# Four weight sums per pair of a three-stage FFN, made by VectorE between its low parts instead of by accumulating DMAs

## The chip, the cores and the metric

The kernel runs on one core of one Trainium2 chip. The metric is the device time of one execution in microseconds (us), the median of several runs. Beside it stands one profiled execution of the same kernel, from which all rows come. A core has TensorE (matmuls, in PSUM), VectorE and ScalarE (element by element), GpSimd (POOL) and SyncE (SP), each with an instruction list of its own that it works off in order; semaphores are the only order between the lists. Transfers are done by 16 DMA engines.

## The reference

Two transformer-like blocks on 512 tokens of width 2048, in FP32. The first is a mixer of pooling and a state space model, the second an attention block with a gated FFN. The change lies in that FFN alone:

```python
D_MODEL, SEQ = 2048, 512
D_FF = -(-8 * D_MODEL // (3 * 256)) * 256          # 5632

h = rmsnorm_2(x, g_pre_ffn[l]) * (1.0 + sc_f) + sh_f
f = (jax.nn.silu(h @ w_gate[l]) * (h @ w_up[l])) @ w_down[l]
x = x + gt_f * rmsnorm_2(f, g_post_ffn[l])
```

## The kernel before

**Tiling.** `D_FF` is 44 tiles of 128 hidden channels. For each tile the kernel needs 128 columns of `w_gate` (g) and of `w_up` (u), each as a RAW tile of 128 x 2048 (16 blocks of 128 input channels). The first two tiles (`PLAIN`) are computed directly. The other 42 (`FAST`) take g and u as the two columns of a 2 x 2 block matrix (input channels in two halves of 1024, tokens in two halves of 256) and use the seven-product scheme of fast matrix multiplication: 7 products of 128 x 1024 weights instead of 8. One such tile is called a pair here, since it has a gate and an up part.

**Seven weights of a pair.** `weight(s2, j)` gives them. With g1, g2, u1, u2 for the halves of g and u they are: 0: g1; 1: sum 3 = g1 + u1; 2: sum 1 = u1 + u2 (made in place of u1); 3: g2; 4: sum 2 = sum 3 + u2; 5: u2; 6: sum 4 = g2 + sum 2 (made in place of g2). The sums' numbers are those of the names `sum_1` to `sum_4` in the code. Two RAW buffers alternate between even and odd pairs.

**High and low parts.** TensorE multiplies at reduced precision (`fp32r`), so each weight is split. ScalarE makes the high part (`hi_part`, line 1177, into `QH`), VectorE the low part (`lo_part`, line 2618, weight minus high part, into `QL`). There are four slots. The high part of weight j + 3 may start when product j - 1 is done (`q_done`), since it takes that product's slot; it also waits for its sum. The low part waits for the high part (`q_hi`), and TensorE's product waits for the low part (`q_lo`).

**Products.** On TensorE (`fast_pair`, lines 1749 and 1751) each product is 8 times a matmul of 512 columns with the high part and one of 256 columns with the low part. Banks of PSUM are shared by products: product 3 goes into the bank of product 0 after ScalarE copied that (`p1_copied`, line 1181), product 5 into that of product 1, and product 6 into that of product 2, after VectorE's subtraction `r` (line 2639) has read it (`taken`).

**VectorE's list for a pair s**, in its order: low part of weight 5; low part of 6; `r` (2639); low part of weight 0 of pair s + 1; low part of 1; line 2642, a drain, line 2644; low part of 2; line 2647; low part of 3; line 2651, a drain, line 2654 (the sum of the gate part, which ScalarE's silu waits for), line 2655 (the sum of the up part); low part of weight 4 of pair s + 1; a drain; line 2661, the multiply into `FO`. ScalarE's list after the high part of weight 3: silu (`gated`, line 1190), the copy of product 0 of the next pair, the high part of weight 4, then of 5, a copy of product 1.

**Sums before.** GpSimd issues them as accumulating DMAs: a DMA with `accum_op=ALU.add` adds its source onto its destination in SBUF. `sum_3` adds u1 onto a `SUMS` tile into which SP had loaded g1 a second time from HBM (0.5 MB); `sum_1` adds u2 onto u1; `sum_2` waits until the low part of weight 1 is made, and `sum_4` until that of weight 3 is. ScalarE's high parts 1, 2, 4 and 6 wait for `first_sums` and `later_sums`.

**Before and after the pairs.** At the start, VectorE also makes the low parts of the combined tokens (`TA`, `TB`, `TC`) and the `FO` multiply of the second plain tile (`plain_hidden(1)`, line 2613), on whose `out_read` TensorE's first product waits. After the pairs comes the multiplication with `w_down` (lines 1779 to 1781).

Of the kernel before, what the change touches and what calls it, by code (L numbers as in the profile page):

```python
# [24 lines left out]
P = 128  # L25
# [125 lines left out]
def build(nc, w_units, w_ada, c_row, x_t, p_t, vec_d, con_d, mask_d, ssm_par, ssm_bc, w_pool_d,  # L151
# [117 lines left out]
    QL = at("QL", 32 * K, [P, 4, FULL_K * P], FP32R)  # L269
    SUMS = [at("SUM0", T0 + 9696, [P, FULL_K * P]), at("SUM1", T0 + 3040, [P, FULL_K * P])]  # L270

# [20 lines left out]
    def weight(s2, j):  # L292

        g, u, h = RAWS[s2][:, 0, :], RAWS[s2][:, 1, :], FULL_K * P
        return [g[:, 0:h], SUMS[s2][:, :], u[:, 0:h], g[:, h:2 * h], SUMS[s2][:, :], u[:, h:2 * h], g[:, h:2 * h]][j]

# [6 lines left out]
    with ExitStack() as ctx:  # L303
        PS = ctx.enter_context(nc.psum_tensor("PS", [P, 8, S], FP32))

        def sem(name):
# [46 lines left out]
        pair_loaded = [sem("pair_loaded0"), sem("pair_loaded1")]  # L353
        first_sums, later_sums, q_hi, q_lo, q_done, copied, taken = (
            sem(n) for n in ("first_sums", "later_sums", "q_hi", "q_lo", "q_done", "copied", "taken"))
        t_sum, t_hi, t_lo, gate_summed, up_summed, silu_done, f_made = (
# [10 lines left out]
        def _(sp):  # L367
# [80 lines left out]
            for k in (1, 0):  # L448
                sp.dma_start(RAWS[1][:, k, :], w_units[U_FFN + 2 * PLAIN + 2 + k]).then_inc(pair_loaded[1], 16)
            sp.dma_start(SUMS[0][:, :], w_units[U_FFN + 2 * PLAIN, :, 0:FULL_K * P]).then_inc(pair_loaded[0], 16)  # L450
            for k in range(2):
# [3 lines left out]
            hidden_saved(0, f_d[0], 0)  # L455
            sp.wait_ge(f_made, PLAIN)
            sp.dma_start(SUMS[1][:, :], w_units[U_FFN + 2 * PLAIN + 2, :, 0:FULL_K * P]).then_inc(pair_loaded[1], 16)
            with sp.Fori(0, LOOPED // 4) as i:
                for e in range(4):
                    for k in (1, 0):  # L460

                        sp.wait_ge(q_lo, 28 * i + (Q0 + PRODUCTS * e + 7 - k))
                        sp.dma_start(RAWS[e % 2][:, k, :], w_units[bass.ds(8 * i + (U_FFN + 2 * PLAIN + 2 * e + 4 + k), 1)]
                                     .rearrange("a p n -> p (a n)")).then_inc(pair_loaded[e % 2], 16)
                    sp.dma_start(SUMS[e % 2][:, :], w_units[bass.ds(8 * i + (U_FFN + 2 * PLAIN + 2 * e + 4), 1), :, 0:FULL_K * P]
                                 .rearrange("a p n -> p (a n)")).then_inc(pair_loaded[e % 2], 16)
                    hidden_saved(4 * i + (e + 1), f_d[bass.ds(4 * i + (e + 1), 1)].rearrange("a p n -> p (a n)"),
                                 (e + 1) % 2)
# [43 lines left out]
        def _(gp):  # L512
# [76 lines left out]
            def sum_1(s, r):

                u = RAWS[r][:, 1, :]
                gp.wait_ge(first_sums, 32 * s + 16)
                gp.dma_start(u[:, 0:h], u[:, h:2 * h], accum_op=ALU.add).then_inc(first_sums, 16)

            def sum_2(s, r):

                gp.wait_ge(q_lo, PRODUCTS * s + (Q0 + 2))
                gp.dma_start(SUMS[r][:, :], RAWS[r][:, 1, h:2 * h], accum_op=ALU.add).then_inc(later_sums, 16)

            def sum_4(s, r):  # L600

                gp.wait_ge(q_lo, PRODUCTS * s + (Q0 + 4))
                gp.wait_ge(later_sums, 32 * s + 16)
                gp.dma_start(RAWS[r][:, 0, h:2 * h], SUMS[r][:, :], accum_op=ALU.add).then_inc(later_sums, 16)

            def weight_sums(s, e, loaded):

                r, n = e % 2, (e + 1) % 2
                sum_2(s, r)
                gp.wait_ge(first_sums, 32 * s + 32)  # L610
                sum_3(n, loaded)
                sum_4(s, r)
                sum_1(s + 1, n)

            sum_3(0, 48)
            sum_1(0, 0)
            for s in range(FAST - 1):
                weight_sums(s, s % 2, 48 * ((s + 1) // 2 + 1))
            sum_2(LOOPED + 1, 1)
            sum_4(LOOPED + 1, 1)  # L620

# [213 lines left out]
        def _(act):  # L835
# [334 lines left out]
            def hi_part(s, s2, j, slot, done):  # L1170

                act.wait_ge(q_done, done)
                if j in (1, 2):
                    act.wait_ge(first_sums, 32 * s + 16 * j)
                if j in (4, 6):
                    act.wait_ge(later_sums, 32 * s + 16 * (j // 2 - 1))
                act.activation(QH[:, slot, :], weight(s2, j), ACT.Copy).then_inc(q_hi, 1)  # L1177
# [55 lines left out]
            plain_silu(1)  # L1233
            act.wait_ge(pair_loaded[0], 48)
            for j in range(2):
# [12 lines left out]
            with act.Fori(0, LOOPED // 4) as i:  # L1248
                for e in range(4):
                    fast_pair(4 * i + e, e, 96 * i + 48 * ((e + 1) // 2 + 1))  # L1250
            fast_pair(LOOPED, 0, 48 * (LOOPED // 2 + 1))
            fast_pair(LOOPED + 1, 1, 0, False)
# [534 lines left out]
        def _(v):  # L1787
# [834 lines left out]

            def fast_pair(s, e, saved, more=True):
                s2, n2, b0 = e % 2, (e + 1) % 2, 4 - 4 * (e % 2)
# [65 lines left out]
            for t in range(FULL_K):  # L2690
                m = 3 * DT + FULL_K + t
                ins = v.scalar_tensor_tensor(out=TC[:, t, hi], in0=RES[:, FULL_K + t, hi], scalar=MOD[:, m:m + 1],
                                             in1=f32(TC[:, t, lo]), op0=ALU.add, op1=ALU.subtract)
            ins.then_inc(t_lo, 1)
            lo_part(0, 0, 3, 3)
            lo_part(0, 0, 4, 0)
            with v.Fori(0, LOOPED // 4) as i:
                for e in range(4):
                    fast_pair(4 * i + e, e, 32 * i + 16 * (e // 2 + 1))
            fast_pair(LOOPED, 0, 8 * LOOPED + 16)  # L2700
            fast_pair(LOOPED + 1, 1, 8 * LOOPED + 16, False)

# [193 lines left out]
```

## Time and profile before

| | us |
|---|---|
| median of 3 runs | 3140.84 |
| lowest and highest | 3133.31, 3145.36 |
| profiled execution | 3136.03 |
| its span in the trace | 3134.3 |
| TensorE busy | 3078.4 |
| VectorE busy | 2070.9 |
| ScalarE busy | 1157.4 |
| mean granted clock of TensorE | 0.992 |

The profile gives each engine's busy time, the instructions in order of time with their start, duration and the idle time ahead of them, and for each idle time what ended it. "PE" is TensorE, "DVE" VectorE, "ACT" ScalarE, "POOL" GpSimd. A duration runs from start to the last write; the next instruction of the same engine can start a little before it ends, so that the step from start to start is what counts in a full list. The granted clock is the share of 2.4 GHz that TensorE gets; 0.5 is 1.2 GHz.

### The profile page before, as it was taken

The page shows a single profiled execution, that of the slowest core. Times are in us where ns is not written, and L with a number is a line of the kernel's source. Part 1 is how long each engine was busy: PE and PEld are TensorE (multiplying, and loading weights), DVE is VectorE, ACT ScalarE, POOL GpSimd, SP SyncE. Part 2 cuts the span into 40 slices and gives each one's busy share as a digit, 9 for nine tenths or more (in the row PEclk, how much of TensorE's full clock was granted, in tenths as well). Part 3 has the DMA queues.
Part 4 walks back from the last instruction along what each step waited for, and adds up shares of the span by engine and source line. Part 5 has one row for each costly group of instructions (what it writes and reads, how often), then busy time and mean ns, then how long its engine had stood idle before and what let it go on. Part 6 is the DMA issues. An engine that isn't in the chain of part 4 may idle for free.

```text
span 3134.3 us, 41612 instructions
## 1 busy us (share of the span) xinstructions
PE 3078.4 (98%) x15416; PEld 2569.8 (82%) x15416; DVE 2070.9 (66%) x2743; ACT 1157.4 (37%) x1522; POOL 417.0 (13%) x589
## 2 busy tenths in 40 slices
PE   8999999999999999999999899999999998999998
PEld 7888877888878888888787688888888887888887
DVE  6666556868885444555788866666666666666665
ACT  5323343213233333444623444444444443222223
POOL 0111100111100000000011311111111111122113
PEclk9999999999999999999999899999999999999999
DMA  4444454875752222222386499999999997455544
GB/s 187 145 136 122 127 194 178 297 270 211 272 226 92 82 81 75 75 80 80 121 304 232 158 238 251 265 252 251 251 250 250 252 254 212 173 187 187 188 166 170
DMA packets 136410, 591.07 MB, mean 189 GB/s; under 512 B 24096, under 2 KB 24368, under 8 KB 99056
## 3 DMA queue, kind: packets, MB, share of 16 engines
q1 hardware_dynamic: 69968, 343.18, 30.7%
q0 software_dynamic: 62448, 218.45, 26.5%
q10 hardware_dynamic: 3888, 28.03, 2.3%
q8 instruction: 67, 1.10, 0.1%
q14 instruction: 39, 0.32, 0.0%
HBM read 457.19 MB, written 37.76 MB: 158 GB/s over the span
## 4 chain that ended last, share of the span: by engine, by line
PE 95%; DVE 3%; DVEq 0%; DMA 0%; ACT 0%; issue 0%; SPq 0%; ACTq 0%
PE PS L1749 18%; PE PS L1329 15%; PE PS L1331 15%; PE PS L1330 15%; PE PS L1751 9%; PE PS L1779 5%; PE PS L1781 5%; PE PS L1780 5%; PE PS L1598 1%; PE PS L1625 1%; PE PS L1382 1%; PE PS L1383 1%; PE PS L1384 1%; PE PS L1613 1%; PE PS L1495 0%; PE PS L1454 0%
## 5 line engine op out<-in xcount | busy, mean ns | idle before, releaser
L1329 PE MATMUL PS<-XHL,WH 128*128 128x512 f32 x1968 | 775.2, 394 | 5.6 <-DVE WL L1791 2.6
L1331 PE MATMUL PS<-XHL,WL 128*128 128x512 f32 x1968 | 766.2, 389 | 0.0
L1330 PE MATMUL PS<-XHL,WH 128*128 128x512 f32 x1968 | 766.0, 389 | 0.0
L839 ACT ACTIVATE WH<-RAW 128x2048 fp32r<-128x2048 f32 x138 | 263.9, 1912 | 522.0 <-PE PS L1331 513.7
L1329 PEld LDWEIGHTS PS<-XHL,WH 128*128 128x128 f32 x1968 | 369.4, 188 | 94.1 <-issue 13.7
L1331 PEld LDWEIGHTS PS<-XHL,WL 128*128 128x128 f32 x1968 | 369.4, 188 | 77.4
L1330 PEld LDWEIGHTS PS<-XHL,WH 128*128 128x128 f32 x1968 | 369.5, 188 | 77.0 <-issue 2.2
L1791 DVE TENSOR_TENSOR WL<-RAW,WH 128x2048 fp32r<-128x2048 f32 x138 | 316.5, 2294 | 79.8 <-ACT WH L839 79.7
L1749 PE MATMUL PS<-XHL,QH 128*128 128x512 f32 x1008 | 361.6, 400 | 2.7 <-DVE FO L2613 2.7
L2618 DVE TENSOR_TENSOR QL<-RAW,QH 128x1024 fp32r<-128x1024 f32 x210 | 257.0, 1224 | 110.4 <-ACT QH L1177 110.4
L1177 ACT ACTIVATE QH<-RAW 128x1024 fp32r<-128x1024 f32 x210 | 221.3, 1058 | 259.7 <-PE PS L1751 231.2
L1751 PE MATMUL PS<-XHL,QL 128*128 128x256 f32 x1008 | 283.8, 282 | 0.0
L1779 PE MATMUL PS<-WH,FH 128*128 128x512 f32 x704 | 274.9, 391 | 8.6 <-issue 8.6
L1780 PE MATMUL PS<-WL,FH 128*128 128x512 f32 x704 | 274.8, 390 | 0.0
L1781 PE MATMUL PS<-WH,FL 128*128 128x512 f32 x704 | 274.8, 390 | 0.0
L1749 PE MATMUL PS<-TA,QH 128*128 128x512 f32 x672 | 239.3, 399 | 0.0
L1749 PEld LDWEIGHTS PS<-XHL,QH 128*128 128x128 f32 x1008 | 190.1, 189 | 50.6 <-issue 3.1
L1826 DVE CUSTOM_DVE_ANT_0 ADA<-ADA,CB 128x1024 f32<-128x1024 f32 x192 | 226.1, 1221 | 5.8 <-DMA ADA<-w_ada_dram 5.8
L1262 ACT ACTIVATE WH<-RAW 128x2048 fp32r<-128x2048 f32 x44 | 84.2, 1915 | 336.5 <-PE PS L1781 336.5
L1751 PEld LDWEIGHTS PS<-XHL,QL 128*128 128x128 f32 x1008 | 191.2, 190 | 0.0
L2618 DVE TENSOR_TENSOR QL<-SUM,QH 128x1024 fp32r<-128x1024 f32 x84 | 102.9, 1225 | 132.3 <-ACT QH L1177 132.3
L1751 PE MATMUL PS<-TA,QL 128*128 128x256 f32 x672 | 188.7, 281 | 0.0
(369 smaller groups left out, 4603.4 us busy)
## 6 DMA issues: line engine op xcount, KB each, us to landing
RAW<-w_units_dram SPq DMA_DIRECT2D x268, 1024.0 KB, 4.9
ADA<-w_ada_dram POOLq DMA_DIRECT2D x192, 512.0 KB, 5.5
SUM<-RAW POOLq DMA_DIRECT2D x84, 512.0 KB, 5.1
SUM<-w_units_dram SPq DMA_DIRECT2D x42, 512.0 KB, 7.4
RAW<-RAW POOLq DMA_DIRECT2D x42, 512.0 KB, 5.3
RAW<-SUM POOLq DMA_DIRECT2D x42, 512.0 KB, 4.6
FR<-f_dram SPq DMA_DIRECT2D x11, 1024.0 KB, 5.5
spill_dram<-SIG POOLq DMA_DIRECT2D x24, 256.0 KB, 2.3
```

Source lines behind the costliest of these rows:

```text
L839: act.activation(WH[:, slot, :], RAW[:, slot, :], ACT.Copy).then_inc(hi_ready, 1)
L1329: pe.matmul(PS[:, bank, :], wh, rh[:, x, :], start=k == 0, stop=False)
L1330: pe.matmul(PS[:, bank, :], wh, rl[:, x, :], start=False, stop=False)
L1331: ins = pe.matmul(PS[:, bank, :], wl, rh[:, x, :], start=False, stop=k == n - 1)
L1749: pe.matmul(in_halves(PS[:, bank, :]), wh, x, start=k == 0 and j not in (3, 5, 6), stop=False, skip_group_check=True)
L1751: ins = pe.matmul(PS[:, bank, 0:HALF_S], wl, x[:, 0, :], start=False, stop=k == FULL_K - 1, skip_group_check=True)
L1779: pe.matmul(PS[:, 4 + n % 4, :], fh, wh, start=k == 0, stop=False, skip_group_check=True)
L1780: pe.matmul(PS[:, 4 + n % 4, :], fh, wl, start=False, stop=False, skip_group_check=True)
L1781: ins = pe.matmul(PS[:, 4 + n % 4, :], fl, wh, start=False, stop=k == FF_CHUNK - 1, skip_group_check=True)
L1791: v.tensor_tensor(WL[:, slot, :], RAW[:, slot, :], f32(WH[:, slot, :]), ALU.subtract)\
L1826: v.tensor_tensor_reduce(ADA[slot][:, :], ADA[slot][:, :], CB[:, :], 1.0, 0.0, ALU.mult, ALU.add, (MODH if half else MOD)[:, t:t + 1]).the ...
L2618: v.tensor_tensor(QL[:, slot, :], weight(s2, j), f32(QH[:, slot, :]), ALU.subtract).then_inc(q_lo, 1)
```

## The change

The accumulating DMAs on GpSimd and the second load of g1 on SP are gone. VectorE makes the four sums as `tensor_tensor` adds of 128 x 1024: `sum_4` behind the low part of weight 5, `sum_3` of the next pair behind that of 6, `sum_1` behind the next pair's 0, `sum_2` behind the next pair's 2. Both sum tiles are now shared by all pairs: `SUM3` holds g1 + u1, and `SUM2`, which was summed in place, is a tile of its own. One semaphore `sum_ready` takes the place of two. In pair 0, `sum_3` and `sum_1` stand ahead of the low parts 0 and 1, and `sum_2` behind the token parts `TC`. The loads' count per buffer falls from 48 to 32.

```diff
+NEED_SUM = {1: 1, 2: 2, 4: 3, 6: 4}
-    SUMS = [at("SUM0", T0 + 9696, [P, FULL_K * P]), at("SUM1", T0 + 3040, [P, FULL_K * P])]
+    SUM3 = at("SUM3", T0 + 9696, [P, FULL_K * P])
+    SUM2 = at("SUM2", T0 + 3040, [P, FULL_K * P])
...
-                    sp.dma_start(SUMS[e % 2][:, :], w_units[bass.ds(8 * i + (U_FFN + 2 * PLAIN + 2 * e + 4), 1), :, 0:FULL_K * P]
-                                 .rearrange("a p n -> p (a n)")).then_inc(pair_loaded[e % 2], 16)
...
-            def sum_3(r, loaded):
-
-                g, u = RAWS[r][:, 0, :], RAWS[r][:, 1, :]
-                gp.wait_ge(pair_loaded[r], loaded)
-                gp.dma_start(SUMS[r][:, :], u[:, 0:h], accum_op=ALU.add).then_inc(first_sums, 16)
...
-            for s in range(FAST - 1):
-                weight_sums(s, s % 2, 48 * ((s + 1) // 2 + 1))
...
             def hi_part(s, s2, j, slot, done):
 
                 act.wait_ge(q_done, done)
-                if j in (1, 2):
-                    act.wait_ge(first_sums, 32 * s + 16 * j)
-                if j in (4, 6):
-                    act.wait_ge(later_sums, 32 * s + 16 * (j // 2 - 1))
+                if j in NEED_SUM:
+                    act.wait_ge(sum_ready, 4 * s + NEED_SUM[j])
...
+            def sum_3(r, loaded):
+                v.wait_ge(pair_loaded[r], loaded)
+                v.tensor_tensor(SUM3[:, :], RAWS[r][:, 0, 0:FULL_K * P], RAWS[r][:, 1, 0:FULL_K * P], ALU.add)\
+                 .then_inc(sum_ready, 1)
+
+            def sum_1(r):
+                u, h = RAWS[r][:, 1, :], FULL_K * P
+                v.tensor_tensor(u[:, 0:h], u[:, 0:h], u[:, h:2 * h], ALU.add).then_inc(sum_ready, 1)
+
+            def sum_2(r):
+                v.tensor_tensor(SUM2[:, :], SUM3[:, :], RAWS[r][:, 1, FULL_K * P:], ALU.add).then_inc(sum_ready, 1)
+
+            def sum_4(r):
+                a12 = RAWS[r][:, 0, FULL_K * P:]
+                v.tensor_tensor(a12, a12, SUM2[:, :], ALU.add).then_inc(sum_ready, 1)
...
+                    if j == 2:
+                        sum_4(s2)
+                    if j == 3 and more:
+                        sum_3(n2, loaded)
+                    if j == 4 and more:
+                        sum_1(n2)
+                    if j == 6 and more:
+                        sum_2(n2)
...
             v.tensor_tensor(TB[:, :, hi], RES[:, b, lo], f32(TB[:, :, lo]), ALU.subtract).then_inc(t_lo, 1)
+            sum_3(0, 32)
+            sum_1(0)
             for j in range(2):
                 lo_part(0, 0, j, j)
             plain_hidden(1)
...
             ins.then_inc(t_lo, 1)
+            sum_2(0)
             lo_part(0, 0, 3, 3)
```

## Rows read from the trace of the kernel before

**Rows 1.** The page's first part: busy time of each engine.

```profile
PE 3078.4 (98%) x15416; PEld 2569.8 (82%) x15416; DVE 2070.9 (66%) x2743; ACT 1157.4 (37%) x1522; POOL 417.0 (13%) x589
```

**Rows 2.** TensorE's instructions in order of time: start us, us, engine, line, operation.

```profile
1802.46 0.69 PE L1749 MATMUL PS<-XHL,QH 128*128 128x512 f32 x1 [2.70 <-DVE FO L2613]
...
1806.91 0.40 PE L1749 MATMUL PS<-TA,QH 128*128 128x512 f32 x1
...
2202.65 0.40 PE L1749 MATMUL PS<-TA,QH 128*128 128x512 f32 x1
...
2635.01 0.28 PE L1751 MATMUL PS<-XHL,QL 128*128 128x256 f32 x1
```

**Rows 3.** The waits from 1802 to 2640 us, TensorE's (all of them).

```profile
PE PS L1749 <- DVE FO L2613: 2.7, 1, 2.7
```

**Rows 4.** Busy time of each engine in one stretch, with the header.

```profile
core 0: us, PE busy (x) PEld busy (x) DVE busy (x) ACT busy (x) POOL busy (x), PEclk, DMA share, GB/s
1806.80:2634.80 828.00, 828.00 (x4689) 717.96 (x4688) 563.44 (x626) 385.61 (x457) 143.45 (x169) 1.00 0.96 251
```

**Rows 5.** VectorE's instructions in order of time, one pair in mid-stretch.

```profile
2201.11 1.23 DVE L2618 TENSOR_TENSOR QL<-RAW,QH 128x1024 fp32r<-128x1024 f32 x1 [0.93 <-ACT QH L1177]
2202.25 0.68 DVE L2651 TENSOR_TENSOR ST<-PS,ST 128x512 f32<-128x512 f32 x1
2203.11 0.69 DVE L2654 TENSOR_TENSOR ST<-ST 128x512 f32<-128x512 f32 x1 [0.17 <-issue]
...
2205.94 1.23 DVE L2618 TENSOR_TENSOR QL<-SUM,QH 128x1024 fp32r<-128x1024 f32 x1 [1.53 <-ACT QH L1177]
2207.32 0.69 DVE L2661 TENSOR_TENSOR FO<-ST 128x512 f32<-128x512 f32 x1 [0.16 <-issue]
2207.93 1.22 DVE L2618 TENSOR_TENSOR QL<-RAW,QH 128x1024 fp32r<-128x1024 f32 x1
2209.67 1.23 DVE L2618 TENSOR_TENSOR QL<-RAW,QH 128x1024 fp32r<-128x1024 f32 x1 [0.52 <-ACT QH L1177]
2210.82 0.68 DVE L2639 TENSOR_TENSOR ST<-ST,PS 128x512 f32<-128x512 f32 x1
...
2216.47 0.68 DVE L2642 TENSOR_TENSOR ST<-PS,ST 128x512 f32<-128x512 f32 x1
2217.24 0.69 DVE L2644 TENSOR_TENSOR ST<-ST 128x512 f32<-128x512 f32 x1
```

**Rows 6.** ScalarE's instructions in order of time, the same pair.

```profile
2203.83 0.64 ACT L1190 ACTIVATE ST<-ST 128x512 f32<-128x512 f32 x1 [2.75 <-DVE ST L2654]
2204.37 0.58 ACT L1181 ACTIVATE ST<-PS 128x512 f32<-128x512 f32 x1
2204.85 1.05 ACT L1177 ACTIVATE QH<-SUM 128x1024 fp32r<-128x1024 f32 x1
```

**Rows 7.** DMA issues: count, KB each, median us from issue to landing.

```profile
RAW<-w_units_dram SPq DMA_DIRECT2D x268, 1024.0 KB, 4.9
```

**Rows 8.** VectorE's instructions in order of time, ahead of the first product.

```profile
1799.16 1.22 DVE L2618 TENSOR_TENSOR QL<-RAW,QH 128x1024 fp32r<-128x1024 f32 x1
1800.29 1.22 DVE L2618 TENSOR_TENSOR QL<-SUM,QH 128x1024 fp32r<-128x1024 f32 x1
1801.43 0.68 DVE L2613 TENSOR_TENSOR FO<-PS,SIG 128x512 f32<-128x512 f32 x1
```

**Rows 9.** Busy time in three short stretches, columns as in rows 4.

```profile
732.00:736.00 4.00, 4.00 (x18) 3.31 (x19) 4.00 (x5) 2.66 (x2) 0.00 (x0) 1.00 0.01 4
740.00:744.00 4.00, 4.00 (x20) 3.30 (x19) 1.21 (x3) 0.94 (x2) 1.06 (x2) 1.00 0.94 312
1802.00:1806.00 4.00, 3.54 (x11) 3.06 (x12) 2.55 (x6) 2.48 (x4) 0.66 (x1) 0.57 0.63 139
```

**Rows 10.** TensorE's instructions in order of time, behind another stop.

```profile
731.84 0.50 PE L1329 MATMUL PS<-XHL,WH 128*128 128x512 f32 x1 [1.46 <-DVE BB L2266]
```

**Rows 11.** Line 2618, plain weights: shortest/median/longest ns, first and last start.

```profile
L2618 DVE TENSOR_TENSOR QL<-RAW,QH x210: 1216/1225/1228, 1799.2 to 2625.4; 128x1024 fp32r<-128x1024 f32 x105
```

More of the change, by code:

```diff
@@ L294, in weight @@
         g, u, h = RAWS[s2][:, 0, :], RAWS[s2][:, 1, :], FULL_K * P
-        return [g[:, 0:h], SUMS[s2][:, :], u[:, 0:h], g[:, h:2 * h], SUMS[s2][:, :], u[:, h:2 * h], g[:, h:2 * h]][j]
+        return [g[:, 0:h], SUM3[:, :], u[:, 0:h], g[:, h:2 * h], SUM2[:, :], u[:, h:2 * h], g[:, h:2 * h]][j]
     def f32(ap):
@@ L353, in build @@
         pair_loaded = [sem("pair_loaded0"), sem("pair_loaded1")]
-        first_sums, later_sums, q_hi, q_lo, q_done, copied, taken = (
-            sem(n) for n in ("first_sums", "later_sums", "q_hi", "q_lo", "q_done", "copied", "taken"))
+        sum_ready, q_hi, q_lo, q_done, copied, taken = (
+            sem(n) for n in ("sum_ready", "q_hi", "q_lo", "q_done", "copied", "taken"))
         t_sum, t_hi, t_lo, gate_summed, up_summed, silu_done, f_made = (
@@ L449, in _ @@
                 sp.dma_start(RAWS[1][:, k, :], w_units[U_FFN + 2 * PLAIN + 2 + k]).then_inc(pair_loaded[1], 16)
-            sp.dma_start(SUMS[0][:, :], w_units[U_FFN + 2 * PLAIN, :, 0:FULL_K * P]).then_inc(pair_loaded[0], 16)
             for k in range(2):
@@ L455, in _ @@
             hidden_saved(0, f_d[0], 0)
-            sp.wait_ge(f_made, PLAIN)
-            sp.dma_start(SUMS[1][:, :], w_units[U_FFN + 2 * PLAIN + 2, :, 0:FULL_K * P]).then_inc(pair_loaded[1], 16)
             with sp.Fori(0, LOOPED // 4) as i:
@@ L579, in _ @@
                 gp.tensor_tensor(BB[:, t, :], BB[:, t, :], RES[:, t, :], ALU.add).then_inc(x3_ready, 1)
-            h = FULL_K * P
-            def sum_3(r, loaded):
-                g, u = RAWS[r][:, 0, :], RAWS[r][:, 1, :]
-                gp.wait_ge(pair_loaded[r], loaded)
-                gp.dma_start(SUMS[r][:, :], u[:, 0:h], accum_op=ALU.add).then_inc(first_sums, 16)
[L589 to L616, printed above, removed]
-            for s in range(FAST - 1):
-                weight_sums(s, s % 2, 48 * ((s + 1) // 2 + 1))
-            sum_2(LOOPED + 1, 1)
-            sum_4(LOOPED + 1, 1)
             def ada_load(n):
@@ L1233, in _ @@
             plain_silu(1)
-            act.wait_ge(pair_loaded[0], 48)
+            act.wait_ge(pair_loaded[0], 32)
             for j in range(2):
@@ L1249, in _ @@
                 for e in range(4):
-                    fast_pair(4 * i + e, e, 96 * i + 48 * ((e + 1) // 2 + 1))
-            fast_pair(LOOPED, 0, 48 * (LOOPED // 2 + 1))
+                    fast_pair(4 * i + e, e, 64 * i + 32 * ((e + 1) // 2 + 1))
+            fast_pair(LOOPED, 0, 32 * (LOOPED // 2 + 1))
             fast_pair(LOOPED + 1, 1, 0, False)
@@ L2621, in both, with fast_pair @@
                 return (ST[:, a, i:i + 2, HALF_S:S] for a in range(2))
-            def fast_pair(s, e, saved, more=True):
+            def sum_3(r, loaded):
[10 more added lines that the diff above has]
+                v.tensor_tensor(a12, a12, SUM2[:, :], ALU.add).then_inc(sum_ready, 1)
+            def fast_pair(s, e, saved, loaded, more=True):
                 s2, n2, b0 = e % 2, (e + 1) % 2, 4 - 4 * (e % 2)
@@ L2698, in _ @@
                 for e in range(4):
-                    fast_pair(4 * i + e, e, 32 * i + 16 * (e // 2 + 1))
-            fast_pair(LOOPED, 0, 8 * LOOPED + 16)
-            fast_pair(LOOPED + 1, 1, 8 * LOOPED + 16, False)
+                    fast_pair(4 * i + e, e, 32 * i + 16 * (e // 2 + 1), 64 * i + 32 * ((e + 1) // 2 + 1))
+            fast_pair(LOOPED, 0, 8 * LOOPED + 16, 16 * LOOPED + 32)
+            fast_pair(LOOPED + 1, 1, 8 * LOOPED + 16, 0, False)
             def down_lo(n):
```

## The prediction

> **What bounds the kernel now.** I began with the busy shares: TensorE is busy for 98% of the span, VectorE for 66% [rows 1]. So time can go only where TensorE stops, and it can come only where something new stops it. The stretch that the change touches is found next, by the first and the last matmul of the fast pairs: they run from 1802.46 to 2635.01 us, 833 of 3134 us for 42 pairs [rows 2]. The list of waits then says what TensorE waited for there: one entry, 2.7 us before the very first product, for the `FO` multiply of VectorE [rows 3]. In the stretch from 1806.8 to 2634.8 us TensorE is busy for all of the 828 us, at a granted clock of 1.00, while VectorE has work for 563 us of them and the DMA engines for 0.96 of their time [rows 4]. Product 1 of the first pair begins at 1806.91, and the last matmul ends at 2635.29 [rows 2]: 828.38 us for 42 x 7 - 1 = 293 products are 2.827 us each, and 19.79 us for a pair. No accumulating DMA is late for TensorE. Taking these DMAs away can therefore give it nothing, and everything hangs on whether VectorE still keeps up.
>
> **Why the busy share misleads.** VectorE is busy for 563.4 / 828 x 19.79 = 13.5 us of a pair [rows 4]; four adds of 1.22 us would make it 18.4, still below 19.8. But VectorE's list is in order, and at two places it must wait for ScalarE. So I laid one pair out, name by name, as a ring of starts, beginning at the GATE add (line 2654) and ending at that of the next pair. The pair shown starts at 2199.82 (its product 1 at 2202.65 [rows 2], less one product), so GATE, at 2203.11, starts 3.29 us into a pair [rows 5].
>
> **Terms that the trace shows.** From GATE to the `lo` of weight 4: 2203.11 to 2205.94, 2.83 us. Inside lie ScalarE's silu, its copy of product 0 and its `hi` of weight 4, end to end [rows 6], and VectorE idles 1.5 us. This piece can't shrink when VectorE is late, for the silu starts 0.03 us after GATE ends. Then `lo` 4 to `FO` 1.38, `FO` to `lo` 5 0.61. Sum 4.82 us [rows 5].
>
> **Sum of weight 6 (sum_4), the one with a price of its own.** It stands behind `lo` 5 and ahead of `lo` 6, and ScalarE's `hi` 6 waits for it, which `lo` 6 waits for in turn. Before, `hi` 6 had its sum from a DMA and waited only for TensorE. Now: `lo` 5 to sum_4 1.14, sum_4 itself 1.22, hand-over 0.03, `hi` 1.06, hand-over 0.04, in all 3.50 us from `lo` 5 to `lo` 6, against 1.74 before [rows 5, 6]. VectorE idles over 1.1 us of it, with everything behind it queued: sum_3, the subtraction `r` (line 2639), on which product 6 waits, and the next pair's low parts.
>
> **The other three sums.** sum_3, sum_1 and sum_2 have no wait of their own that is late: the RAW tiles of the next pair are asked for after `lo` 5 and `lo` 6 of the pair before, about 20 us ahead of sum_3, and land in 4.9 us [rows 7]. The two loads that remain lose only SUM loads ahead of or behind them on SP's queue, which nobody waits for any more. Each sum costs its pitch. No row shows a plain f32 add of 128x1024, but the low part is the same instruction form at the same size, and three VectorE instructions back to back started 1.13 and 1.14 us apart [rows 8]; I take 1.14. The bounds: 1024 columns cost 1.14 and 512 cost 0.61, so 512 more cost 0.53, and an add without any fixed part 1.06; an add that is in nobody's shadow costs its full duration, 1.225 [rows 11].
>
> The Trainium skill, page "VectorE: DVE Perf Modes", section "The DRAIN you can't avoid", says that the next operation does not start until the pipe is empty. By that each full-width step would cost 1.225 and not 1.14, nine of them 0.77 us more per pair, and the result would be some +74 us; rows 8 show the earlier start, so the sum goes by 1.14.
>
> **The rest of the ring.** Full-width steps behind `lo` 6: `lo` 6, sum_3, `lo` 0, sum_1, `lo` 1, `lo` 2, sum_2, `lo` 3, eight times 1.14 = 9.12 us. Narrow steps: `r` 0.61, line 2642 0.77 (with its drain), line 2644 0.61, line 2647 0.61, line 2651 to GATE 0.86, sum 3.46 us [rows 5]. At each of them I looked at whether ScalarE or TensorE is later than VectorE. `hi` 0 to `hi` 3 need products 3 to 6 done and sum_3 or sum_1; all come over 1 us before VectorE gets there. So the ring is 4.82 + 3.50 + 9.12 + 3.46 = **20.90 us**, against TensorE's 19.79. It isn't covered: 1.11 us per pair too long, and TensorE will run at VectorE's pace.
>
> **When it starts to bite.** TensorE's tightest wait is product 6 on `r`: `r` ends 4.82 + 3.50 + 1.14 + 1.14 + 0.69 = 11.29 after GATE, 14.6 into the pair, and product 6 begins at 16.96. That slack of 2.3 us is used up in two or three pairs. Product 3 waits for the copy of product 0, with 3.3 us of slack, and comes second. In the last pair sum_3 is missing, so `r` is 1.14 earlier and the slack that counts is 3.4. From the GATE of pair 0 to that of pair 40 there are 40 rounds: 40 x 1.11 = 44.4, less 3.4 = **+41.0 us**.
>
> **The start.** sum_3 and sum_1 of pair 0 stand ahead of `lo` 0, `lo` 1 and the `FO` multiply, without an idle place between them, and this `FO` is what TensorE's first product waited for [rows 3, 8]. So TensorE starts 2 x 1.14 = **2.3 us** later. sum_2 of pair 0 lies beside product 1. TensorE had stood 2.7 us, the next 4 us had a mean clock of 0.57, most of it at 1.2 GHz [rows 9], and product 0 took 4.45 instead of 2.83 us [rows 2]. A stop of 5 us may lengthen that by up to another 1.3 us. I take nothing for it and keep it for the range.
>
> **The end.** After the last product the chain (line 2651, GATE, silu, `FO`, `FH`, `FL`) is as before; the loads for the next stage are asked for earlier against TensorE's end than is needed. Nothing.
>
> **POOL and DMA.** 168 accumulating DMAs, 0.5 MB each, and 42 SUM loads go. Does anything run faster for it? `lo` took 1216 to 1228 ns with DMA at 0.96 [rows 4, 11], so VectorE isn't slowed by it; and TensorE issued 18 matmuls in 4 us with DMA at 0.01 and 20 with 0.94 [rows 9]. Nothing, with a bound of 0.01 us per full-width step.
>
> **Sum.** +41.0 + 2.3 = +43.3 us. The profiled execution took 3136.0 us (span 3134.3), which is 4.8 below the median of the runs, 3140.8. So it gives 3179.3 from the profile, 3184 from the median; I say **3181 us**.
>
> **Rivals.**
> (a) *The adds are hidden* (the other side, not slower). Place: the two idle stretches of VectorE, 1.5 and 1.1 us. Price: only the start, +2.3 us, 3138 to 3143. It decides at a ring of 19.79 us, so 1.11 us would have to be missing: four adds of 0.86 instead of 1.14 each, or a `hi` 6 that overlapped sum_4. For it stands that VectorE has 265 us without work in 828 [rows 4]; against it that the wait list gives the order, and that no instruction of this kind and width is under 1.2 us [rows 11]. 7%.
> (b) *The clock falls.* The ring makes TensorE stand about 1.1 us per pair, split between product 6 and product 3. If each stop brought as much of the low clock as the start had, a pair would lose the 1.6 us that product 0 lost, and TensorE would need 21.4 us for it, 0.5 more than the ring: up to 42 x 0.5 = 21 us more, 3185 to 3205. Against it: a stop of 1.46 us at 731.84 was followed by a clock of 1.00; for it: after 2.7 us it fell [rows 9, 10]. 6%.
> (c) *Less DMA makes TensorE or its feeders quicker*, with the ring short enough to let it through: 3115 to 3125. TensorE never waits for DMA, so only its pace could gain, and rows 9 show none. 2%.
> (d) *A longer ring*: an unseen wait of 0.1 to 0.3 us per pair (semaphore hand-over for the new waits in ScalarE, loop branch in VectorE, which today hides in the idle places), 4 to 12 us more: 3185 to 3196. 20%. The change not doing what it says is part of this: if sum_3 did wait for its load on VectorE, all behind it would wait as well; 20 us against 4.9 speaks against it.
>
> **Chances.** The forecast with its own range of 3172 to 3190: 65%; (d) 20%; (a) 7%; (b) 6%; (c) 2%. A tenth of a us in the ring is 4 us in the result, and the runs of before lie 12 us apart. The range of 8 in 10 takes in the forecast and most of (d): 3165 to 3196. A measurement of this kernel can tell about 0.5%, 15.7 us, from no change. Slower by more: the forecast, (d) and (b), 91%; same: (a), 7%; faster: 2%.
>
> **What would show it.** TensorE's wait list gets a new entry, line 1749 for `ST` of line 2639, about 40 times 0.8 to 1.1 us, perhaps a smaller one for ScalarE's copy (line 1181); TensorE's busy time stays, its share falls to about 97%. VectorE's list shows about 1.1 us of idle before `lo` 6 and 1.5 us before `lo` 4, none elsewhere, and GATE adds 20.9 us apart. The first product starts near 1804.8 us. If the GATE adds stay 19.8 us apart, the ring is wrong and (a) holds; if TensorE's clock in the stretch is under 0.98, (b) does.

## The result, and the profile after

The changed kernel takes 3177.54 us (median, 3177.13 to 3178.21), beside 3138.16 for the kernel before in the same job: +39.4 us by the medians (1.3%). The ratio estimated from all the executions is 1.0112, with an interval of 1.0092 to 1.0132; every ratio below is meant in this way, against the kernel before in the same job. The forecast was 3181 us, from +43.3. The profiled execution after took 3177.13 us with a span of 3175.4, 41.1 more than before.

The page's first line, of after, answers to [rows 1]: TensorE's busy time is 10 us up and its share down by a point, VectorE gains 178 us, POOL loses 143.

```profile
PE 3088.3 (97%) x15416; PEld 2566.6 (81%) x15416; DVE 2248.4 (71%) x2911; ACT 1149.1 (36%) x1522; POOL 273.8 (9%) x421
```

TensorE's waits (engine and line, whom for: us in total, times, longest), of after; `L1703` is the product's matmul (1749 before), `L2617` the subtraction `r` (2639), `L2567` the `FO` multiply (2613). Against [rows 3] the first entry is new, and the last has grown from 2.7 to 5.0. The middle one stands behind the pairs, where the multiplication with `w_down` begins; the kernel before has it too, with the same 8.6 us.

```profile
PE PS L1703 <- DVE ST L2617: 29.2, 37, 1.0
...
PE PS L1733 <- issue: 8.6, 1, 8.6
...
PE PS L1703 <- DVE FO L2567: 5.0, 1, 5.0
```

The busy time of the engines over the pairs, of after, columns as in rows 4. VectorE works 733 of 863 us (before 563 of 828), the DMA share is 0.33 instead of 0.96, and the clock is still 1.00.

```profile
1812.00:2675.00 863.00, 833.07 (x4659) 710.53 (x4658) 732.91 (x785) 374.72 (x455) 1.36 (x3) 1.00 0.33 114
```

VectorE's instructions in order of time, of after, one round of the ring; it answers to [rows 5]. `L2572` is a low part, `L2632` GATE, `L2639` `FO`, `L2591` sum_4, `L2579` sum_3, `L2617` `r`.

```profile
2204.63 0.69 DVE L2632 TENSOR_TENSOR ST<-ST 128x512 f32<-128x512 f32 x1 [0.16 <-issue]
...
2207.46 1.23 DVE L2572 TENSOR_TENSOR QL<-SUM,QH 128x1024 fp32r<-128x1024 f32 x1 [1.53 <-ACT QH L1131]
2208.98 0.69 DVE L2639 TENSOR_TENSOR TMP<-ST 128x512 f32<-128x512 f32 x1 [0.30 <-issue]
2209.59 1.22 DVE L2572 TENSOR_TENSOR QL<-RAW,QH 128x1024 fp32r<-128x1024 f32 x1
2210.73 1.22 DVE L2591 TENSOR_TENSOR RAW<-RAW,SUM 128x1024 f32<-128x1024 f32 x1
2213.08 1.23 DVE L2572 TENSOR_TENSOR QL<-RAW,QH 128x1024 fp32r<-128x1024 f32 x1 [1.13 <-ACT QH L1131]
2214.22 1.22 DVE L2579 TENSOR_TENSOR SUM<-RAW 128x1024 f32<-128x1024 f32 x1
2215.36 0.68 DVE L2617 TENSOR_TENSOR ST<-ST,PS 128x512 f32<-128x512 f32 x1
...
2225.60 0.69 DVE L2632 TENSOR_TENSOR ST<-ST 128x512 f32<-128x512 f32 x1 [0.16 <-issue]
```

Read it so: from the low part at 2209.59 to the one at 2213.08 it is 3.49 us, with sum_4 between and then 1.13 us of idle time in which ScalarE makes the high part 6. The other place without work is the 1.53 us ahead of 2207.46. There is no third of more than 0.3 us. GATE to GATE is 20.97 us here, 20.82 for the pair before, and 834.9 / 40 = 20.87 on average, from 1828.83 (pair 0) to 2663.75 (pair 40). ScalarE's own row shows who it waited for, and TensorE's row the stop that this makes at product 6:

```profile
2211.98 2.01 ACT L1131 ACTIVATE QH<-RAW 128x1024 fp32r<-128x1024 f32 x2 [3.12 <-DVE RAW L2591]
```

```profile
2216.09 0.50 PE L1703 MATMUL PS<-XHL,QH 128*128 128x512 f32 x1 [0.82 <-DVE ST L2617]
```

**Where the 41.1 us of the two traces are.** From the first matmul of the pairs to the end of the last: before 2635.29 - 1802.46 = 832.8, after 2677.14 - 1803.00 = 874.1, +41.3 us. The stop ahead of them: 2.70 to 4.97, +2.3. What lies ahead of that stop was 1.7 us shorter in this execution and what lies behind the pairs 0.7 shorter. I put both down to scatter: in before_again_1 below, a second trace of the unchanged kernel, the first matmul of the pairs comes at 1804.44 and not at 1802.46. Sum 41.2, for the 41.1 of the spans.

### The profile page after: what moved, and what is told of

Its sections match the earlier page's. It is cut to its first block, busy times and chain, and to the rows that moved or that the text cites. A ratio compares the mean times of both kernels' runs of the same rounds, so it can differ in the third digit from the quotient of the medians.

```text
span 3175.4 us, 41477 instructions
## 1 busy us (share of the span) xinstructions
PE 3088.3 (97%) x15416; PEld 2566.6 (81%) x15416; DVE 2248.4 (71%) x2911; ACT 1149.1 (36%) x1522; POOL 273.8 (9%) x421
## 4 chain that ended last, share of the span: by engine, by line
PE 69%; DVE 19%; DVEq 5%; issue 4%; ACT 3%; DMA 0%; ACTq 0%
PE PS L1283 15%; PE PS L1285 14%; PE PS L1284 14%; DVE QL L2572 7%; PE PS L1733 5%; PE PS L1735 5%; PE PS L1734 5%; ACT QH L1131 3%; DVEq L2621 2%; DVEq L2630 2%; DVE SUM L2579 2%; DVE RAW L2591 1%; DVE SUM L2587 1%; PE PS L1552 1%; PE PS L1579 1%
## 5 line engine op out<-in xcount | busy, mean ns | idle before, releaser
L1703 PE MATMUL PS<-XHL,QH 128*128 128x512 f32 x1008 | 367.4, 406 | 34.9 <-DVE ST L2617 29.2
L2572 DVE TENSOR_TENSOR QL<-RAW,QH 128x1024 fp32r<-128x1024 f32 x210 | 256.1, 1220 | 49.6 <-ACT QH L1131 49.5
L1131 ACT ACTIVATE QH<-RAW 128x1024 fp32r<-128x1024 f32 x210 | 213.7, 1053 | 206.5 <-DVE RAW L2591 126.3
L1703 PEld LDWEIGHTS PS<-XHL,QH 128*128 128x128 f32 x1008 | 190.2, 189 | 98.6 <-DVE ST L2617 40.3
L1703 PE MATMUL PS<-TA,QH 128*128 128x512 f32 x672 | 237.7, 397 | 0.0
L2701 DVE TENSOR_TENSOR RES<-RES,PS 128x512 f32<-128x512 f32 x160 | 106.7, 686 | 109.3 <-PE PS L1735 104.0
```

The source lines that it names most:

```text
L1703: pe.matmul(in_halves(PS[:, bank, :]), wh, x, start=k == 0 and j not in (3, 5, 6), stop=False, skip_group_check=True)
L2572: v.tensor_tensor(QL[:, slot, :], weight(s2, j), f32(QH[:, slot, :]), ALU.subtract).then_inc(q_lo, 1)
```

## The experiments

All are of the changed kernel unless it is said otherwise.

**sum4_in_idle.** One instruction moved.

```diff
-                    if j == 2:
-                        sum_4(s2)
...
                 if more:
+                    sum_4(n2)
                     lo_part(s + 1, n2, 4, (PRODUCTS * e + PRODUCTS + 4) % 4)
...
             lo_part(0, 0, 3, 3)
+            v.drain()
+            sum_4(0)
             lo_part(0, 0, 4, 0)
```

> Of the changed kernel, with one instruction moved: sum_4 of the next pair stands behind the UP add (line 2655 of before), where VectorE stands idle for 1.5 us waiting for ScalarE's high part 4, instead of between the low parts 5 and 6. Same adds, same number, same bytes. Theory (the order of VectorE's list, a ring of 20.87 us as the trace of after shows it against 19.79 of TensorE): sum_4 then costs nothing where it stands (1.14 us in a gap that has 1.5), the high part 6 no longer waits for it, and the step from low part 5 to 6 falls from 3.5 to 1.14 us: a ring of 18.5 us, TensorE bound again, no entry of line 1703 for the subtraction r; only the start's 2.3 us are left: about 3141 us, ratio 1.001. Rival 1 (VectorE has too much work, or adds are slow beside ScalarE's reads): the work is the same, so 3170 to 3178. Rival 2 (the loss is a fixed share, half of it the width of the add and half of it the wait): 3155 to 3160.

Measured: 3137.99 us (median of 10, 3122.49 to 3143.14), ratio 0.9975, 0.9955 to 0.9996. The same work in another order takes back all of the loss and more. VectorE's rows (`L2630` GATE, `L2591` sum_4) show the sum inside the old gap, 0.40 us of it left:

```profile
2200.65 0.69 DVE L2630 TENSOR_TENSOR ST<-ST 128x512 f32<-128x512 f32 x1 [0.17 <-issue]
2201.26 0.68 DVE L2631 TENSOR_TENSOR ST<-ST 128x512 f32<-128x512 f32 x1
2201.86 1.22 DVE L2591 TENSOR_TENSOR RAW<-RAW,SUM 128x1024 f32<-128x1024 f32 x1
2203.49 1.23 DVE L2572 TENSOR_TENSOR QL<-SUM,QH 128x1024 fp32r<-128x1024 f32 x1 [0.40 <-ACT QH L1131]
```

Rivals 1 and 2 fall. But 3138 is no good summary: four of the ten executions lie at 3122 to 3125, six at 3138 to 3143. That is taken up below.

**sum4_before_lo5.** sum_4 one place earlier, so that only the wait goes, not the width.

```diff
                 for j in range(2, PRODUCTS):
+                    if j == 2:
+                        sum_4(s2)
                     if j + 3 < PRODUCTS:
                         lo_part(s, s2, j + 3, (PRODUCTS * e + j + 3) % 4)
                     elif more:
                         lo_part(s + 1, n2, j - 4, (PRODUCTS * e + j + 3) % 4)
-                    if j == 2:
-                        sum_4(s2)
```

> Of the changed kernel, with sum_4 one place earlier: ahead of the low part 5 instead of behind it. It takes away only the wait of the high part 6 for the sum (the low part 5 now runs beside it), not the 1.14 us of the add. Theory: ring 20.87 - (3.50 - 2.28) = 19.65 us, just under TensorE's 19.79: nearly all of the loss gone, 3140 to 3145 us; VectorE has almost no idle time left but the 1.5 us ahead of low part 4. Rival (the add's width is what costs, not the wait): at most half is won back, 3155 to 3175 us.

Measured: 3136.38 us (3132.82 to 3142.01), ratio 0.9978, 0.9963 to 0.9994. GATE adds are 19.79 us apart, TensorE's number; the low parts 5 and 6 stand back to back behind the sum:

```profile
2207.99 0.69 DVE L2632 TENSOR_TENSOR ST<-ST 128x512 f32<-128x512 f32 x1 [0.17 <-issue]
...
2212.82 1.22 DVE L2591 TENSOR_TENSOR RAW<-RAW,SUM 128x1024 f32<-128x1024 f32 x1
2213.95 2.44 DVE L2572 TENSOR_TENSOR QL<-RAW,QH 128x1024 fp32r<-128x1024 f32 x2
...
2227.78 0.69 DVE L2632 TENSOR_TENSOR ST<-ST 128x512 f32<-128x512 f32 x1 [0.17 <-issue]
```

So the 1.1 us for which VectorE stands while ScalarE makes the high part 6 are what pushed the ring over the edge. A ring worked out at 19.65 held against 19.79: nothing is left of the loss in this trace.

**sum2_twice.** One add more per pair.

```diff
                     if j == 6 and more:
+                        v.tensor_tensor(SUM2[:, :], SUM3[:, :], RAWS[n2][:, 1, FULL_K * P:], ALU.add)
+                        v.drain()
                         sum_2(n2)
```

> Of the changed kernel, with one add more: sum_2 is made twice in each of 41 pairs, with a drain between. Same result. Theory (VectorE's list sets the pace, each us in it is a us of the pair): 1.14 + 0.16 us (the drain as at line 2642) more per pair, 40 x 1.30 = 52 us: 3229 us, GATE adds 22.2 us apart, TensorE's stops 2.4 us per pair. Rival (part of the time comes from elsewhere and VectorE has some slack): under 3215. If stops of about 2.4 us in a pair lower TensorE's clock, its products take longer in the records but the pace is still VectorE's, no more than 3229.

Measured: 3232.28 us (3231.77 to 3233.30), ratio 1.0288, 54.7 over the changed kernel where 52 were expected. GATE adds 22.1 us apart, 1.27 more:

```profile
2252.59 0.69 DVE L2634 TENSOR_TENSOR ST<-ST 128x512 f32<-128x512 f32 x1 [0.17 <-issue]
2274.71 0.69 DVE L2634 TENSOR_TENSOR ST<-ST 128x512 f32<-128x512 f32 x1 [0.16 <-issue]
```

41 adds with their drains cost 1.3 us each: VectorE has no slack left. TensorE's stops divide between the two places that the prediction named, product 3 (ScalarE's copy, `L1135`) and product 6 (`r`), and the clock over 788 us stays at 1.00.

```profile
PE PS L1703 <- ACT ST L1135: 47.7, 40, 1.7
PE PS L1703 <- DVE ST L2619: 30.1, 39, 0.9
```

```profile
1812.00:2600.00 788.00, 721.60 (x4009) 611.78 (x4008) 674.41 (x711) 324.16 (x394) 0.00 (x0) 1.00 0.32 108
```

**r_first.** The instruction that the wait list blames, made earlier.

```diff
-                    if j == 3 and more:
-                        sum_3(n2, loaded)
...
                         v.tensor_tensor(r, r, bank(2), ALU.subtract).then_inc(taken, 1)
+                        if more:
+                            sum_3(n2, loaded)
```

> Of the changed kernel, with the subtraction r (line 2639 of before), on which TensorE's product 6 waits by the wait list, moved ahead of sum_3, so 1.14 us earlier. Theory: r isn't in the ring as a cause, the ring stays 20.87 us; TensorE only gets its slack once more, so 1.1 us in the whole kernel: 3176.5 us, with the stop moved from product 6 to another place (product 3, for ScalarE's copy, or a low part). Rival (the wait that the list names is the cause, and an earlier r cures it): 1.1 us per pair is won, 3135 to 3145 us.

Measured: 3178.87 us (3177.59 to 3179.53), ratio 1.0116: nothing is won, not even the 1.1 us that were expected once. TensorE now waits somewhere else, at product 3 for ScalarE's copy:

```profile
PE PS L1703 <- ACT ST L1135: 35.9, 38, 1.2
```

The wait list tells at which instruction a late list is felt, not what makes it late.

**sum2_four_times.** Of the changed kernel, with three adds more, each with a drain; one execution.

```diff
                     if j == 6 and more:
+                        v.tensor_tensor(SUM2[:, :], SUM3[:, :], RAWS[n2][:, 1, FULL_K * P:], ALU.add)
+                        v.drain()
+                        v.tensor_tensor(SUM2[:, :], SUM3[:, :], RAWS[n2][:, 1, FULL_K * P:], ALU.add)
+                        v.drain()
+                        v.tensor_tensor(SUM2[:, :], SUM3[:, :], RAWS[n2][:, 1, FULL_K * P:], ALU.add)
+                        v.drain()
                         sum_2(n2)
```

> Of the changed kernel, with sum_2 made four times per pair, a drain behind each of the first three. Theory (ring): 3 x 1.30 us more per pair, 24.8 us from GATE to GATE, 40 x 3.9 = 156 us: 3334 us. TensorE stands some 5 us per pair in two stops (products 3 and 6). If a stop of this length lowers its clock, the products after it take longer and use up part of the stops, but the time stays 3334 us, as VectorE sets it; the granted clock of the stretch falls under 0.9. Rival (the low clock adds to the ring): over 3345 us.

Measured: 3340.2 us in the one execution, 6 over the sum. Stops of 3.7 and 3.8 us now stand at product 3. TensorE's rows show one of 3.8 us with the low clock behind it (first matmul 0.79 us long) and one of 2.1 us without (0.49); over the stretch the clock is 0.93, not under 0.9 as expected.

```profile
1885.23 0.79 PE L1703 MATMUL PS<-XHL,QH 128*128 128x512 f32 x1 [3.82 <-ACT ST L1135]
...
2207.07 0.49 PE L1703 MATMUL PS<-XHL,QH 128*128 128x512 f32 x1 [2.10 <-ACT ST L1135]
```

```profile
1812.00:2600.00 788.00, 687.67 (x3599) 588.87 (x3598) 682.19 (x700) 291.21 (x349) 0.00 (x0) 0.93 0.28 96
```

GATE adds lie 24.7 to 24.8 us apart, as the ring has it, so the low clock used up stops. Of the 6 us, 3.9 are no cost of the clock: the three adds are made in 41 pairs, and the sum counted 40. That leaves some 3 us as the most that the low clock can have cost.

**no_accumulate.** Of the kernel before: the function bodies and calls of the four DMA sums on GpSimd go, and the waits for them. Nothing makes the sums, so the products use the unsummed weights; the second load of g1 stays.

```diff
-            sum_3(0, 48)
-            sum_1(0, 0)
-            for s in range(FAST - 1):
-                weight_sums(s, s % 2, 48 * ((s + 1) // 2 + 1))
-            sum_2(LOOPED + 1, 1)
-            sum_4(LOOPED + 1, 1)
...
-                if j in (1, 2):
-                    act.wait_ge(first_sums, 32 * s + 16 * j)
-                if j in (4, 6):
-                    act.wait_ge(later_sums, 32 * s + 16 * (j // 2 - 1))
```

> Of the kernel before, with the removing part of the change alone: the 168 accumulating DMAs on GpSimd and the waits for them are left out, and nothing makes the sums (weights 1, 2, 4 and 6 are the unsummed tiles; SP still loads the SUM tiles). Theory (no transfer was late for TensorE): the same, 3138 to 3141 us, ratio 0.998 to 1.001, DMA share in the stretch down from 0.96 to about 0.35. Rival (the DMAs' traffic slows TensorE's pace; the kernel with sum_4 in the idle place had 4 of 10 executions at 3122 to 3125 us, and its trace a pace of 346.7 ns per two matmuls where the kernel before has 353.4): a good part of its executions lies at 3120 to 3128 us, median lower by 5 us or more.

Measured: 3135.12 us (3119.44 to 3137.84, 12 executions), ratio 0.9966, 0.9950 to 0.9982. This is where the prediction was wrong: the DMAs cost about 0.3%, 11 us by the means and 7 by the medians. The executions are in two heaps, four at 3119 to 3122, eight at 3134 to 3138; the kernel before had 18 in the same job, all from 3134 to 3150.

**The two heaps are two paces of TensorE.** Each product is eight couples of matmuls, one of 512 and one of 256 columns. I took the starts of the 512-column ones from the trace and averaged their distances over each stretch without a stop. In the low heap (the profiled execution of sum4_in_idle) it is 346.7 ns over 2342 couples on end, in the high one (that of sum4_before_lo5) 353.3 ns over 2341; 2352 couples times 6.6 ns are 15.5 us, the distance of the heaps. The durations show it too (shortest/median/longest ns of the 512-column matmuls of product 4), of sum4_in_idle and then of sum4_before_lo5:

```profile
L1703 PE MATMUL PS<-TC,QH x336: 391/391/391, 1820.0 to 2618.4; 128*128 128x512 f32 x168
```

```profile
L1703 PE MATMUL PS<-TC,QH x336: 395/398/403, 1820.2 to 2633.9; 128*128 128x512 f32 x168
```

None of the ten executions of sum4_before_lo5 lies in the low heap, and its ring says why. At the quick pace a pair takes TensorE 56 x 0.3467 = 19.41 us, which is the distance of the GATE adds in sum4_in_idle, and the ring of 19.65 would then be the longer one. By this estimate it lasts 40 x 0.24 = 9.6 us longer than the low heap of sum4_in_idle, 3132 to 3135 us, and five of its ten executions lie there. Its one trace had the slow pace, so this isn't shown.

In the changed kernel, which stops twice per pair, the pace is drawn anew at the restarts: of its stretches of ten couples or more 33 had the quick pace and 42 the slow one, with one between. No matter for its time, since VectorE sets that: the changed kernel's executions lie within 1.1 us, those of before within 12 in the same job.

**stops_with_accumulate, stops_no_accumulate.** Do the accumulating DMAs forbid the quick pace? Of the kernel before and of no_accumulate (again without the sums), the same edit, which makes VectorE late:

```diff
                     if j == 5:
                         v.wait_ge(q_done, q + 5)
+                        for _ in range(8):
+                            v.tensor_tensor(staged(ST_V), bank(1), staged(ST_P1), ALU.subtract)
+                            v.drain()
                         v.tensor_tensor(staged(ST_V), bank(1), staged(ST_P1), ALU.subtract).then_inc(taken, 1)
```

> Of the kernel before, accumulating DMAs and all, with the V subtraction (line 2642) made nine times per pair, a drain behind each of the first eight (8 x 0.77 = 6.2 us). Same result. VectorE's ring becomes about 15.1 + 6.2 = 21.3 us, so TensorE has to stop in nearly every pair and takes its pace anew some 80 times. Theory A (the pace, 346.7 or 353.3 ns per two matmuls, is drawn at each restart whatever the DMAs do): near half of the stretches between stops are quick, as in the changed kernel (33 of 75). Theory B (accumulating DMAs keep TensorE in the slow pace, which is why the kernel before had no execution under 3133 us in 41): none or few are quick. Time by the ring: 3137 + 40 x 1.5 = about 3197 us in either case.

> Of no_accumulate (no accumulating DMAs, sums not made), the same nine V subtractions. Ring 21.3 us, about 3197 us. By both theories near half of the stretches between stops are quick; it is the partner that differs from stops_with_accumulate in the accumulating DMAs alone. If fewer than a quarter are quick here too, the DMAs aren't the difference and this pair settles nothing.

Measured: 3203.08 and 3196.76 us, one execution each. Both have the same line in TensorE's waits, here with the DMAs (the line is 1704 and 1136 in the other):

```profile
PE PS L1749 <- ACT ST L1181: 49.4, 41, 1.3
```

Of 42 stretches 26 were quick with the accumulating DMAs and 28 without. Theory B falls: with accumulating DMAs the quick pace is as frequent, as far as 42 stretches of one execution each can tell.

**before_again_1, before_again_2.** The kernel before, two more traces.

> The kernel before, unchanged, for a second trace: its executions lie from 3133 to 3152 us, against 3134 to 3138 for the slower half of no_accumulate. Theory B (accumulating DMAs): TensorE's pace in the pairs is 353.3 ns throughout, and what is over 3136 us lies in that stretch, as stops or as slower matmuls. Theory A: it is 346.7 in one of two or three executions.

> As before_again_1, a third trace of the kernel before, for the same question: is the spread of its time (3133 to 3152 us) in the stretch of the pairs or ahead of it, and is the pace 353.3 ns again.

Measured: 3153.26 and 3159.89 us. Neither theory had this: the kernel before does stop for its DMAs, only not in the execution that was profiled. The waits from 1802 to 2665 us, of before_again_1:

```profile
ACT QH L1177 <- DMA RAW<-SUM: 133.6, 39, 4.4
ACT QH L1177 <- DMA RAW<-RAW: 86.2, 30, 5.2
...
ACT QH L1177 <- DMA SUM<-RAW: 39.9, 26, 2.4
...
PE PS L1749 <- DVE ST L2639: 9.8, 12, 1.2
```

and of before_again_2:

```profile
ACT QH L1177 <- DMA RAW<-SUM: 149.2, 42, 5.7
ACT QH L1177 <- DMA RAW<-RAW: 89.7, 33, 5.6
...
ACT QH L1177 <- DMA SUM<-RAW: 54.9, 32, 3.0
...
PE PS L1749 <- DVE ST L2639: 15.3, 15, 2.7
```

ScalarE waited 260 and 294 us for sums by DMA, half of it for sum 4 (RAW<-SUM), ahead of the same high part 6. In the trace of the prediction the same three lines were:

```profile
ACT QH L1177 <- DMA RAW<-SUM: 26.8, 11, 2.9
ACT QH L1177 <- DMA SUM<-RAW: 11.3, 8, 2.2
ACT QH L1177 <- DMA RAW<-RAW: 4.5, 4, 1.7
```

43 us, and none reached TensorE. The DMA for sum 1 landed in 8.4 and 8.5 us (median) in the two new traces and in 5.3 in the old one, at a DMA share of 0.93 to 1.01 in all three. A stop can bring a new draw of the pace, and both new traces have stretches of either pace. The first 45 us of before_again_1 were quick and ended in a stop. So a plausible reading is that a quick TensorE runs into its own late sums and so no execution of before stays quick to the end (none of 44 was under 3133 us). This wasn't tested: before_again_2 began with the slow pace and stopped as well.

The traces do show where sum 4 loses its time, and it is little in the DMA itself. Its median from issue to landing was 5.3 and 5.6 us in the two new traces, against 4.6. But it was issued 8.1 and 7.9 us (median) after the first matmul of its pair, against 2.9. In GpSimd's list `sum_3` of the next pair stands ahead of it, and waits for the second load of g1. GpSimd's waits for that load, of before_again_1, of before_again_2 and of the trace of the prediction:

```profile
POOL SUM L587 <- DMA SUM<-w_units_dram: 220.7, 38, 8.1
```

```profile
POOL SUM L587 <- DMA SUM<-w_units_dram: 207.0, 34, 7.4
```

```profile
POOL SUM L587 <- DMA SUM<-w_units_dram: 95.8, 39, 6.8
```

The trace of the prediction was no different at first: in its first eight pairs sum 4 was issued 6.1 to 7.8 us into the pair, and from the twelfth on at about 3. In before_again_1 it came down to 3 only in the last three pairs. Since the loads are asked for behind the low parts 5 and 6, and high part 6 waits for sum 4, a late sum 4 makes the next load late too, so that lateness can be handed from pair to pair. This is a reading of issue times, not an experiment; why one execution catches up and the next doesn't is open, and no run separates the second load from the adds by DMA.

**start_reordered.** Of sum4_in_idle, the start in another order on ScalarE and VectorE. The diff is against the changed kernel and shows the start alone.

```diff
+            act.wait_ge(out_done, O_FFN + 2 * PLAIN)
+            hi_part(0, 0, 2, 2, 1)
+            hi_part(0, 0, 3, 3, 1)
             act.wait_ge(t_lo, 3)
...
-            act.wait_ge(out_done, O_FFN + 2 * PLAIN)
-            hi_part(0, 0, 2, 2, 1)
-            hi_part(0, 0, 3, 3, 1)
...
+            plain_hidden(1)
+            lo_part(0, 0, 0, 0)
             sum_3(0, 32)
             sum_1(0)
-            for j in range(2):
-                lo_part(0, 0, j, j)
-            plain_hidden(1)
+            lo_part(0, 0, 1, 1)
             lo_part(0, 0, 2, 2)
+            sum_2(0)
+            lo_part(0, 0, 3, 3)
+            v.drain()
+            sum_4(0)
             v.wait_ge(t_hi, 4)
...
-            sum_2(0)
-            lo_part(0, 0, 3, 3)
             lo_part(0, 0, 4, 0)
```

> Of sum4_in_idle, with the start reordered: the FO multiply on which the first product waits stands first on VectorE, then low part 0, sum_3, sum_1, low parts 1 and 2, sum_2, low part 3, sum_4, the token parts; ScalarE makes the high parts 2 and 3 ahead of its token parts. Theory: TensorE's stop ahead of the first product falls from 5.0 to about 1.6 us and product 0 no longer runs at the low clock (4.5 to 5.3 us before, then 2.8), with some 0.5 us of new stops in the products 1 to 4: 5 us less than sum4_in_idle at equal pace, 3133 to 3136 us. Rival (product 0 stays at the low clock, or the low parts 1 to 4 come late): 3138 to 3142. If TensorE takes one of two paces (346.7 or 353.4 ns) when it restarts after a stop, this kernel may also have its 15 us lower executions, as often or not.

Measured: 3121.38 us (median of 7, 3118.56 to 3136.36), ratio 0.9948, 0.9928 to 0.9968, the quickest of all, and quicker than both kernels. The stop is 2.28 us and not 1.6, since `FO` now waits for the plain product itself. The clock held at 1.00 (the first matmul takes 0.49 us and not 0.79), and two small stops follow, the first of them at product 1:

```profile
1802.88 0.49 PE L1703 MATMUL PS<-XHL,QH 128*128 128x512 f32 x1 [2.28 <-DVE QL L2572]
1806.43 0.49 PE L1703 MATMUL PS<-TA,QH 128*128 128x512 f32 x1 [0.51 <-DVE QL L2572]
```

Heap by heap its medians are 3 to 5 us under those of sum4_in_idle, which ran in another job (3118.6 to 3121.4 against 3122.5 to 3125.1, and 3133.9 to 3136.4 against 3137.8 to 3143.1). That its median lies in the low heap, with four executions of seven there against four of ten, is the luck of the draw as far as these runs can tell.

## Why the prediction was right, and where it was wrong

**What bounds it, and the busy share.** Right: 13.5 + 4.9 us of work in a pair of 19.8 looked harmless and wasn't. The order of the list decided, as sum4_in_idle and sum4_before_lo5 show: the same adds, 40 us less.

**The ring.** 20.90 us forecast, 20.87 measured. `lo` 5 to `lo` 6: 3.50 and 3.49. GATE to `lo` 4: 2.83 and 2.83. sum_3 to `r`: 1.14 and 1.14, which settles the pitch of an add that no row of before had; the duration of 1.22 us is not what an add costs in a full list. The passage of the Trainium skill that the prediction cites, in "VectorE: DVE Perf Modes", section "The DRAIN you can't avoid", itself goes on to say that a next operation which isn't held starts earlier, and these starts fit that. The terms of the prediction's sum_4 piece add up to 3.49 and not 3.50. Rounds take 20.82 to 20.86 us but for every fourth, where the idle time ahead of one `FO` multiply is 0.30 us, once 0.53, and not 0.16 to 0.19, and the round 20.97, once 21.20. The loop is unrolled by four pairs, so that is most likely its branch, the small cost held as case (d).

**When it bites.** 44.4 less 3.4 = +41.0 forecast, +41.3 measured from first to last matmul. Product 6 was the first wait and ScalarE's copy the second, as said. The stops at product 6 were 0.8 us on average and not up to 1.1; a part stands at product 3, which began up to 0.2 us late in 18 pairs, too little for an entry in the wait list.

**The start.** +2.3 forecast, 4.97 - 2.70 = +2.3 measured. Product 0 took 5.3 us (1803.00 to 1808.28) instead of 4.45, so the longer stop did lengthen the low clock by 0.8 us; it cost nothing, VectorE being late anyhow.

**POOL and DMA.** Wrong. "Nothing" was read from one execution that happened to have no late sum. The removal alone is worth 0.3% (no_accumulate), by stops that go and by a quick pace that can then last. My rival (c) had the sign right and got 2%, and its places, TensorE's pace under DMA traffic, were the wrong ones: no run shows a pace that depends on the traffic. It didn't show in the result because a ring of VectorE's list doesn't care how quick TensorE is. That is also why the total came out: what the sum should have said is not "before plus 43" but "40 rounds of 20.87 us, from a given start".

**The median.** I took 3181, between 3179 from the profiled execution and 3184 from the median. The lower end was the better one, since the executions of before scatter upward by DMA stops which the changed kernel no longer has.

**Rivals.** (a) would have needed the order of sum4_in_idle. (b) is refuted for this kernel: clock 1.00 with stops up to 1.0 us, and still 1.00 with stops up to 1.7 us in sum2_twice.

## What to carry to other kernels

When work is moved onto an engine that is "66% busy", lay out one round of its list with the hand-overs to the other engines; the sum of starts, not the busy share, is to be compared with the bound, and one instruction between a producer and its consumer can cost more than its width. Look for a place where the engine stands idle anyway and put the work there: the same four adds were free. And read more than one execution before writing that a transfer is never late: a wide scatter of the times is a sign that a wait comes and goes.

## What the runs showed of the hardware

- TensorE ran the same list of matmuls at one of two paces, 346.7 or 353.3 ns per couple of 512 and 256 columns, at a granted clock of 1.00 in both. It was taken at a restart after a stop and, in the executions without further stops, held for more than 800 us. Over the six kernels that stop in every pair, 160 stretches were quick and 170 slow. What decides the draw wasn't found; with accumulating DMAs and without them the shares were alike (26 of 42, 28 of 42). It isn't an even draw everywhere: behind the stops at product 6 of sum2_twice 9 of 39 stretches were quick. The pace can also change without a stop that the wait list shows. A stretch of 126 couples in before_again_2 ran at 346 to 347 ns up to its 70th and at 349, 350 and 361 ns in turn behind that. The change lies at the first matmul of product 6, at 1922.15 us, 0.15 us behind the end of `r`, for which that matmul waits.
- Stops of up to 1.7 us in sum2_twice and of 1.85 us in before_again_2 (to 1862.63) left the clock at 1.00. Behind 2.7 us it was low, in the trace of before [rows 9] and in before_again_2 (2.66 us, 0.50 over the 4 us from 2411.2). In between it went either way: 2.28 us in start_reordered and 2.10 and 2.35 us in sum2_four_times (to 2207.07 and 2108.03) left it at 1.00, while 2.31 us (to 2801.40) was followed by a mean of 0.57 over 4 us, from 1 us after the restart. In that kernel it was low at once behind a stop of 3.82 us (to 1885.23), and behind one of 3.74 us (to 2231.79) it fell 0.9 us after the restart and was back within 5 us.
- Full-width VectorE instructions back to back started 1.13 to 1.14 us apart at a duration of 1.22 us, the plain f32 adds as well as the low parts.
